# Queries and keys of ten head pairs made as block products in the gate phase and kept in device memory

## The chip, the cores and the metric

The kernel runs on one core of one Trainium2 chip. The metric is the device time of one execution in microseconds. Before the change three executions took 3416.34, 3417.03 and 3417.95 us, median 3417.03 us.

Names of engines: PE is TensorE, DVE is VectorE, ACT is ScalarE, POOL is GpSimd, SP is SyncE (it only issues DMAs here). Each runs its own instructions in order; they meet at semaphores.

## The reference, cut to what matters

A sequence of 1024 tokens of width 1024 goes through a first block (RWKV-7, mLSTM and a convolved FFN; untouched by the change) and then through two layers of a second block:

```python
h = rmsnorm_2(x, norm_g[layer])
u = h @ w_in[layer]
qa,ka,va,fa,za, qb,kb,vb,zb, qc,kc,vc,zc, ga,gb,gc = split(u)
ya = forgetting_attention(qa, ka, va, log_sigmoid(fa + b))      # 4 heads of 64, causal
ya = ya * silu(za)
yb = dilated_mixture_attention(rope(qb), rope(kb), vb) * silu(zb)   # 6 heads
yc = banded_attention(rope(qc), rope(kc), vc, 127, sinks) * silu(zc)  # 6 query heads on 2
merged = sigmoid(ga)*(ya @ w_br_a) + sigmoid(gb)*(yb @ w_br_b) + sigmoid(gc)*(yc @ w_br_c)
x = x + merged @ w_out[layer]
```

All is float32. The scores are scaled by 1/8 (head width 64).

## The kernel before

**Layout and precision.** Activations lie transposed: 128 channels on the partitions, 1024 tokens along the row, so a 1024-wide tensor is 8 such tiles (`xT`, 4 KB per partition each). A product of full precision is made of three products of halves: each operand is split in a high part (`hH`, `wH`) and the rest (`hL`, `wL`), and `wH*hH`, `wH*hL`, `wL*hH` are added in PSUM. POOL splits each weight tile (`split`, L683: `wH` at L688, `wL` at L690); a split waits until the product that used the buffer before is done.

**Plain column products.** `col_gemm` (L928, matmuls at L943) makes one tile of 128 output channels: 8 tiles of the input, 3 products, 2 halves of 512 tokens = 48 matmuls of 512 columns. It can run pieces of other work between its matmuls (`between`; the key is 3 x input tile + product, two matmuls each).

**Gate phase** (`gate_phase`: PE L1674, ACT L2588, DVE L3587). The 24 tiles of `ga, gb, gc` of a layer are made first: 4 plain, then 20 as `GATE_PAIRS` = 10 pairs. Such a pair takes the two output tiles, the two halves of the input channels and the two halves of the tokens as a 2x2 block product and makes it with 7 block products in place of 8 (`gate_products`, L1632): 7 x 4 tiles x 3 = 84 matmuls of 512 columns (L1650), with weight sums by POOL and ACT (`gate_high` L2541, `gate_low` L834). Per pair, ACT copies a seed (L2561), DVE adds and scales what comes out (L3639 to L3654), ACT applies the sigmoid (L2548), and SP stores the tile into device memory (`keep`). After pair 1 ACT also computes the logarithms of the forget gates (`gate_logs_of`, L2633 and L2635), which needs two other function tables. The block products use the second halves of the rows of `hH` and `hL` 0 to 3 as weight buffers, so ACT and DVE remake these halves after the last pair (L2607, L3670).

**Attention.** Heads are worked on two at a time: pairs A0, A1 (forgetting), B0, B1, B2 (dilated), C0 to C2 (band). A pair of A or B has four column products in PE's queue (`head_pair`, L1823), in the order query, key, value, gate z (the first pair A0: value, query, key, z). The end of the pair before (last transposes, last value products, reciprocal rows) is laid between the matmuls of the query product (`pair_end`, L1807). Between those of the z product lie the value transposes (L1708), the scores of the first 128 queries (`scores(0)`, L1740), and the first three of 8 periods: `period(n)` makes the scores of block n+1, transposes the probabilities of block n (L1767) and multiplies those of n-1 with the values (L1785). DVE takes bias and maximum of each score block (`maxima`, L3811), ACT the exponential (L2689). `period(0)` begins with `scores(1)`, which waits for both maxima of block 0.

**What DVE does ahead of the first maxima of a pair** (L3751), in its order: the output of the pair before (L3874); for A1 query scaling (L3724), scale and low part of the output before (`output_scale` L3736, `output_low` L3742, between them ACT's `yH` L2645), keys (L3730), two masks of the bias rows (L3776), the value copy (L3718). For B: rotary embedding of the query (L3709, L3712, L3714), `output_scale`, `output_low`, that of the keys, the value copy. Ahead of B0 it also scales the rotary tables (L3949, L3953). The half-turned copies that the embedding needs are made by ACT (raw copies L2638) and DMAs within SBUF (L2665). `output_scale` waits for reciprocals that go through device memory (L2657).

**SP's queue** after the gate phase is a plain loop of weight loads (L657).

## Time and profile before

| what | value |
| --- | --- |
| median of three executions | 3417.03 us |
| profiled execution, span from first to last instruction | 3412.5 us |
| what lies around the span, to the median | 4.5 us |
| PE busy | 3254.9 us, 95% |
| DVE, POOL, ACT busy | 58%, 48%, 31% |
| gate phase pairs, both layers | 1510 to 1717 us, 2480 to 2682 us |
| head pairs A0 to B2, both layers | 1717 to 2104 us, 2682 to 3069 us |

A row of a timeline or of the chain is one piece of work with its start and length in microseconds from the start of the span; in brackets stands how long the engine sat idle before it and what ended that. A row of windows gives for a stretch the busy time of each engine with the number of instructions in parentheses, then the granted TensorE clock as a share of 2.4 GHz. Matmul durations overlap: back to back, a 512-column matmul takes less than the duration shown for one.

### The profile page before, as it was taken

To read this page: it belongs to the slowest core of one execution; us is meant where nothing else is said; L and a number is where in the kernel's file an instruction comes from. 1 tells how busy PE (TensorE), PEld (TensorE's weight loads), DVE (VectorE), ACT (ScalarE), POOL (GpSimd) and SP (SyncE) were. 2 spreads that over 40 slices of the span, in tenths; PEclk is the share of its full clock that TensorE was granted. 3 is DMA by queue.
4 is the path that set the end of the run, shared out by engine and by line. 5 is a ranking of instruction groups with operands and counts; after the bars stand their busy time and mean duration, and the time that the engine had idled before them with its cause. 6 is when DMAs were issued, how large, how long until landed. Compare 5 with 4: busy or idle time off the path is not lost.

```text
span 3412.5 us, 55095 instructions
## 1 busy us (share of the span) xinstructions
PE 3254.9 (95%) x22070; PEld 2604.8 (76%) x22070; DVE 1971.0 (58%) x2678; ACT 1055.3 (31%) x1725; POOL 1622.7 (48%) x903
## 2 busy tenths in 40 slices
PE   7999789898999999999999999999999999999997
PEld 6878688687888888787877777678878877776786
DVE  7445644648877777883344554566752256444665
ACT  4212344223323333344332232320343233322301
POOL 3333334146777676657822222257478422222475
PEclk9999899999999999999999999999999999999998
DMA  3121100221111111112331211143223311111332
GB/s 137 44 91 44 56 4 4 85 83 53 53 55 41 54 55 55 50 62 99 143 107 44 56 52 47 38 163 121 99 105 106 119 45 50 43 44 50 136 124 87
DMA packets 88252, 247.68 MB, mean 73 GB/s; under 512 B 13072, under 2 KB 24048, under 8 KB 86144
## 3 DMA queue, kind: packets, MB, share of 16 engines
q1 hardware_dynamic: 69664, 189.34, 16.5%
q10 hardware_dynamic: 18400, 55.63, 5.0%
q8 instruction: 142, 2.33, 0.3%
q14 instruction: 46, 0.38, 0.0%
HBM read 191.28 MB, written 42.12 MB: 68 GB/s over the span
## 4 chain that ended last, share of the span: by engine, by line
PE 85%; DVE 8%; ACT 2%; issue 2%; POOL 2%; DMA 0%; DVEq 0%; POOLq 0%; SPq 0%; ACTq 0%
PE ps L943 30%; PE ps L1480 11%; PE ps L1650 9%; PE ps L1510 6%; PE ps L1934 5%; PE ps L1955 4%; PE ps L1740 3%; PE ps L1767 3%; PE ps L1785 3%; DVE sc L3811 2%; PE ps L1255 1%; PE ps L1533 1%; PE ps L1231 1%; PE ps L1618 1%; POOL unit_lo L834 1%
## 5 line engine op out<-in xcount | busy, mean ns | idle before, releaser
L688 POOL TENSOR_TENSOR wH<-wraw,pv 128x1024 fp32r<-128x1024 f32 x135 | 267.0, 1978 | 1221.5 <-PE ps L943 1097.7
L943 PE MATMUL ps<-hH,wH 128*128 128x512 f32 x1488 | 473.9, 400 | 26.3 <-DVE hL L3041 11.7
L943 PE MATMUL ps<-hL,wH 128*128 128x512 f32 x1488 | 466.6, 395 | 0.0
L943 PE MATMUL ps<-hH,wL 128*128 128x512 f32 x1488 | 465.2, 394 | 0.0
L3368 DVE TENSOR_TENSOR xT<-ps,xT 128x512 f32<-128x512 f32 x544 | 366.1, 690 | 60.9 <-PE ps L1510 54.8
L690 POOL TENSOR_TENSOR wL<-wraw,wH 128x1024 fp32r<-128x1024 f32 x135 | 353.7, 2620 | 10.6
L943 PEld LDWEIGHTS ps<-hH,wH 128*128 128x128 f32 x1488 | 274.5, 189 | 88.8 <-issue 17.9
L943 PEld LDWEIGHTS ps<-hL,wH 128*128 128x128 f32 x1488 | 277.8, 189 | 59.0 <-issue 1.7
L943 PEld LDWEIGHTS ps<-hH,wL 128*128 128x128 f32 x1488 | 277.7, 189 | 57.5 <-issue 0.3
L2689 ACT ACTIVATE sc<-sc,stat 128x256 f32<-128x256 f32 (+7 forms) x256 | 171.1, 669 | 163.1 <-DVE stat L3818 102.1
L1767 PE MATMUL ps<-cst,sc 128*128 128x128 f32 x900 | 148.7, 285 | 12.5 <-ACT pt L2709 8.4
L1767 PEld LDWEIGHTS ps<-cst,sc 128*128 128x128 f32 x900 | 97.0, 141 | 82.8 <-issue 60.7
L1740 PE MATMUL ps<-kP,qP 64*128 64x256 f32 (+3 forms) x672 | 131.6, 488 | 20.4 <-DVE stat L3818 16.6
L1650 PE MATMUL ps<-mixH,unit_hi 128*128 128x512 f32 x320 | 128.7, 402 | 14.5 <-POOL unit_lo L834 7.6
L1480 PE MATMUL ps<-mixH,unit_hi 128*128 128x512 f32 x336 | 133.8, 398 | 7.0 <-DVE ps L3483 4.1
L1480 PE MATMUL ps<-mixH,unit_lo 128*128 128x512 f32 x336 | 132.7, 395 | 0.0
L1480 PE MATMUL ps<-mixL,unit_hi 128*128 128x512 f32 x336 | 132.7, 395 | 0.0
L1650 PE MATMUL ps<-mixL,unit_hi 128*128 128x512 f32 x320 | 127.9, 400 | 0.0
L1650 PE MATMUL ps<-mixH,unit_lo 128*128 128x512 f32 x320 | 127.7, 399 | 0.0
L1785 PE MATMUL ps<-pt,vtok 128*64 128x128 f32 x1800 | 126.5, 280 | 0.0
L1510 PE MATMUL ps<-gL,wH 128*128 128x512 f32 x320 | 126.5, 395 | 0.0
L1510 PE MATMUL ps<-gH,wH 128*128 128x512 f32 x320 | 124.6, 389 | 0.0
(545 smaller groups left out, 7244.0 us busy)
## 6 DMA issues: line engine op xcount, KB each, us to landing
wraw<-ws SPq DMA_DIRECT2D x158, 512.0 KB, 3.5
gates<-gated SPq DMA_DIRECT2D x48, 512.0 KB, 2.7
sg<-gates SPq DMA_DIRECT2D x16, 1536.0 KB, 6.5
upA<-ws SPq DMA_DIRECT2D x42, 256.0 KB, 3.3
upB<-ws SPq DMA_DIRECT2D x42, 256.0 KB, 2.6
gateA<-ws SPq DMA_DIRECT2D x40, 256.0 KB, 3.5
gateB<-ws SPq DMA_DIRECT2D x40, 256.0 KB, 2.7
xT<-park ACTq DMA_DIRECT2D x2, 4096.0 KB, 12.1
```

The costliest lines, as they stand in the source:

```text
L688: pool.tensor_tensor(wH[:, j, :], wraw[:, j, :], zero, ALU.add).then_inc(w_hi, 1)
L690: pool.tensor_tensor(wL[:, j, :], wraw[:, j, :], wH[:, j, :], ALU.subtract).then_inc(w_ready[j], 1)
L943: mm = pe.matmul(pair(p)[:, half * HALF:(half + 1) * HALF], wp, hp[:, k, half * HALF:(half + 1) * HALF], start=(m == 0 and n == 0), stop=( ...
L1480: mm = pe.matmul(bank(b), wp, xp[:, k0 + k, c0:c0 + HALF], start=(start and k == 0 and n == 0), stop=(k == 3 and n == 2), skip_group_check ...
L1510: mm = pe.matmul(pair((2, 3, 1)[e % 3])[:, half * HALF:(half + 1) * HALF], w[:, 1, e * P:(e + 1) * P], h[:, half * HALF:(half + 1) * HALF] ...
L1650: mm = pe.matmul(bank(banks[b]), wp, xp[:, k0 + k, c0:c0 + HALF], start=(start and k == 0 and m == 0), stop=(k == 3 and m == 2), skip_grou ...
L1740: mm = pe.matmul(outs[j][:, c:e], qP[r, n * P:(n + 1) * P], kP[r, k0 + c - c0:k0 + e - c0], start=True, stop=True)
L1767: mm = pe.transpose(out[:, c:c + P], (SC[0] if br == "C" else SC[n % 2])[:, j, b + c:b + c + P], ident)
L1785: mm = pe.matmul(out[r, :], vtok[:, v + 64 * j:v + 64 * j + 64], pt[:, j, b + c:b + c + P], start=(c == c0), stop=(c + P == c1))
L1934: mm = pe.matmul(pair(p)[:, half * HALF:(half + 1) * HALF], wp, hp[:, k, half * HALF:(half + 1) * HALF], start=(k == k0 and n == 0), stop= ...
L2689: act.activation(buf[:, j, b + c0:b + c1], buf[:, j, b + c0:b + c1], ACT.Exp, bias=stat[:, S_NEG, s:s + 1], accum_out=stat[:, S_DEN, s:s + ...
L3368: ins = dve.tensor_tensor(x, bank(2 * pairs[e % len(pairs)] + half), x, ALU.add)
```

## The change

The queries and keys of pairs A0, A1, B0, B1, B2 are no longer plain column products in `head_pair`. They are made as `QK_PAIRS` = 5 more block pairs (one query and one key tile each) ahead of the 10 gate pairs, with the same 7 block products, stored to a tensor `qk` in device memory without the sigmoid, and loaded from there: into `qP` and `kP` for A (already scaled), and for B also, with the halves of each head swapped, into `turned` (four DMAs of 32 partitions each). `load_pair(n)` stands in SP's queue before the weight loads of the next pair and waits until all scores of the pair before are made; the A0 query is loaded during gate pair 1, its key after the last gate. A head pair then has two column products, value and z; the end of the pair before lies between the matmuls of the value product. DVE drops the query and key scaling of A and, for B, does both rotary embeddings first (`rope_loaded`), then `output_scale` and `output_low`. ACT drops its raw copies and in-SBUF swaps, and issues the bias-row DMAs of A0 at the end of the gate phase, ahead of remaking the halves of `hH`. In A0 the masks come before the value copy. In numbers per layer: 10 column products (480 matmuls) go, 35 block products (420 matmuls) come.

```diff
 PLAIN = 4
 GATE_PAIRS = (3 * KT - PLAIN) // 2
+QK_PAIRS = 5
+PAIRS = QK_PAIRS + GATE_PAIRS
 SLOT_GATES = 30
-LAYER_USES = 25
...
+
+    if n < QK_PAIRS:
+        return 2 + 4 * n, 3 + 4 * n
+    return gate_slot_of(PLAIN + 2 * (n - QK_PAIRS)), gate_slot_of(PLAIN + 2 * (n - QK_PAIRS) + 1)
 
...
+            def keep_second(L, n):
+                if n >= QK_PAIRS:
+                    keep(L, PLAIN + 2 * (n - QK_PAIRS) + 1)
+                    return
+                wait(sp, "g_in", L, PLAIN + 2 * n + 2)
+                if n < 2:
+                    wait(sp, "g_scaled", L, scaled(n))
+                else:
...
+
+            def keep_first(L, n):
+                if n >= QK_PAIRS:
+                    keep(L, PLAIN + 2 * (n - QK_PAIRS))
+                    return
+                wait(sp, "g_in", L, PLAIN + 2 * n + 1)
+                sp.dma_start(qk[2 * n], gated[0][:, :]).then_inc(sem("g_kept0"), 16)
+
+            def load_pair(L, n):
...
+
+                sp.wait_ge(sem("at_S"), (L * 8 + n) * 16)
+                for q, (dst, name) in enumerate(((qP, "q_in"), (kP, "k_in"))):
+                    sp.dma_start(dst[:, :], qk[2 * n + q]).then_inc(sem(name), 16)
+                    if n == 2 and q == 0:
+                        sp.wait_ge(sem("at_max"), (L * 8 + 1) * 16 + 18)
+                    if n >= 2:
+                        for a in range(4):
+                            b = a ^ 1
+                            sp.dma_start(turned[q][32 * a:32 * a + 32, :], qk[2 * n + q, 32 * b:32 * b + 32, :]
+                                         ).then_inc(sem(name), 16)
+
...
+                        sp.dma_start(qP[:, :], qk[0]).then_inc(sem("q_in"), 16)
+                    if n + 1 < PAIRS:
                         a, b = part(n + 1)
...
-                keep(L, 3 * KT - 1)
+                        wait(sp, "up_lo", L, PAIRS * UNITS)
+                        raw(1, u + 3, start + 5)
+                    keep_first(L, n)
+                keep_second(L, PAIRS - 1)
+                wait(sp, "g_in", L, PLAIN + 2 * PAIRS)
+                sp.wait_ge(sem("rows_ready"), L * 2 + 2)
+                wait(sp, "g_kept1", L, 16 * 3)
+                sp.dma_start(kP[:, :], qk[1]).then_inc(sem("k_in"), 16)
...
-                with sp.Fori(0, 12) as i:
+                for n in range(1, QK_PAIRS):
                     for j in range(2):
-                        sp.wait_ge(w_ready[j], i + (u + 5))
-                        sp.dma_start(wraw[:, j:j + 1, :], ws[bass.ds(i * 2 + (j + start + 6), 1)].rearrange("s p n -> p s n")
-                                     ).then_inc(raw_full[j], 16)
+                        raw(j, u + 3 + n, start + 4 * n + 4 + j)
+                    if n == 2:
+                        wait(sp, "g_kept0", L, 16 * (2 + PAIRS))
...
                         value_transposes(2)
 
                     def first_scores():
                         if br == "B":
                             pe.wait_ge(sem("a_rope"), L * 10 + i * 2 + 2)
-                        pe.wait_ge(sem("a_raw"), raw + 2)
+                        else:
+                            pe.wait_ge(sem("q_in"), since("q_in", loaded(L, br, i) + 16))
+                            pe.wait_ge(sem("k_in"), since("k_in", loaded(L, br, i) + 16))
                         scores(0)
...
+                    pieces = {4: value_tiles, 5: first_scores, 11: lambda: period(0), 16: lambda: period(1),
+                              21: lambda: period(2)}
...
-                        pe.wait_ge(sem("a_v"), L * 6 + 1)
-                        col_gemm(*slots[1], p=3)
-                        wait(pe, "a_free", L, GATE_PAIRS)
-                        col_gemm(*slots[3], p=1, between={2: value_tiles, 4: first_scores, 17: lambda: period(0),
-                                                          20: lambda: period(1), 22: lambda: period(2)})
...
+                        wait(pe, "g_in", L, PLAIN + 2 * PAIRS - 3)
+                        col_gemm(*slots[0], p=2, between={11: lambda: wait(pe, "half_lo", L, 4)}, first=4)
+                        wait(pe, "b_free", L, PAIRS - 1)
+                        wait(pe, "a_free", L, PAIRS - 1)
+                        col_gemm(*slots[1], p=1, between=pieces)
                     else:
                         col_gemm(*slots[0], p=0, between=ended)
-                        col_gemm(*slots[1], p=1)
-                        pe.wait_ge(sem("a_raw"), raw + 1)
-                        col_gemm(*slots[2], p=0)
-                        pe.wait_ge(sem("a_raw"), raw + 2)
-                        col_gemm(*slots[3], p=1, between={4: value_tiles, 5: first_scores, 11: lambda: period(0),
-                                                          16: lambda: period(1), 21: lambda: period(2)})
+                        col_gemm(*slots[1], p=1, between=pieces)
                 ends_here = br == "C" and i == 2
                 for n in range(within, 8 if ends_here else 7):
...
-                gate_sigmoid(L, PLAIN + 2 * n)
-                if n + 1 < GATE_PAIRS:
+                if n >= QK_PAIRS:
+                    gate_sigmoid(L, PLAIN + 2 * (n - QK_PAIRS))
+                if n + 1 < PAIRS:
...
-                    wait(act, "up_used", L, RING + GATE_PAIRS * UNITS - 3 + q)
+                wait(act, "up_used", L, RING + PAIRS * UNITS - 3)
+                bias_rows(L, 0)
+                for q in range(RING):
+                    k = ring_at(PAIRS - 1, q + 3)
+                    wait(act, "up_used", L, RING + PAIRS * UNITS - 3 + q)
                     act.activation(hH[:, k, HALF:T], xT[:, k, HALF:T], ACT.Copy, scale=norm_weight(L, k)
...
                 else:
                     slots = head_slots(L, br, i)
-                    if br == "B":
-                        act.wait_ge(gemm_done[0], slots[0][1] + 1)
-                        raw = L * 14 + i * 2 + 2 * first
-                        raw_copy(qraw2, 0, 0.125)
-                        swap_halves(qraw2, 0, raw + 1)
-                        output_hi(L, i + (first - 1))
-                        act.wait_ge(gemm_done[1], slots[1][1] + 1)
-                        raw_copy(kraw2, 1)
-                        act.wait_ge(sem("a_rot"), swaps(L, i * 2 + 1))
-                        swap_halves(kraw2, 1, raw + 2)
-                    if br == "A":
-                        for j in range(2):
-                            for q in range(2):
-                                spread(alternate(cM[q][:, j, :], 1 - q),
-                                       alternate(out[2 * i + j:2 * i + j + 1, L, :], 1 - q), L + 3)
+                    if br == "A" and i:
+                        bias_rows(L, i)
                     if br == "A" and i == 0:
                         first_values(L)
-                    if br == "A" and i:
+                    else:
+                        act.wait_ge(gemm_done[slots[0][0]], slots[0][1] + 1)
+                        act.activation(vst2[:, :], pair(0), ACT.Copy).then_inc(sem("a_v"), 1)
                         output_hi(L, i + (first - 1))
-                    if br == "B" or i:
-                        act.wait_ge(gemm_done[slots[2][0]], slots[2][1] + 1)
-                        if br == "B":
-                            act.wait_ge(sem("a_rope"), L * 10 + i * 2 + 1)
-                        act.activation(vst2[:, :], pair(0), ACT.Copy).then_inc(sem("a_v"), 1)
                 def unmask(n):
...
-                    dve.tensor_tensor(ga[:, HALF:T], c, grows[:, HALF:T], ALU.mult).then_inc(sem("g_in"), 1)
+                    exit_first(ga[:, HALF:T], c, 1).then_inc(sem("g_in"), 1)
                     wait(dve, "up_used", L, used + 7)
...
+                    if n < 2 or n >= QK_PAIRS:
+                        dve.tensor_tensor(gb[:, 0:HALF], a, grows[:, 0:HALF], ALU.mult).then_inc(sem("a_free"), 1)
+                    else:
+                        dve.tensor_copy(gb[:, 0:HALF], a).then_inc(sem("a_free"), 1)
                     wait(dve, "a_free", L, n + 1)
                     dve.sem_inc(sem("g_in"), 1)
...
+            def rope_loaded(L, n, q, done):
+
+                step, dst, turn = n * 2 + (L + 1) * 2, (qP, kP)[q][:, :], turned[q][:, :]
+                name = ("q_in", "k_in")[q]
+                dve.wait_ge(sem(name), since(name, done))
+                dve.tensor_tensor(dst, dst, ropeT[:, 0, :], ALU.mult).then_inc(sem("rope_step"), 1)
+                dve.tensor_tensor(turn, turn, ropeT[:, 1, :], ALU.mult).then_inc(sem("rope_step"), 1)
+                dve.wait_ge(sem("rope_step"), step + 2)
+                dve.tensor_tensor(dst, dst, turn, ALU.add).then_inc(sem("a_rope"), 1)
...
-                        queries(L, i)
-                        output_scale(L, i + (first - 1))
-                        output_low(L, i + (first - 1))
-                        keys(L, i)
                 if br == "B":
-                    for q, raw, dst in ((0, qraw2, qP), (1, kraw2, kP)):
-                        rope(L, L * 10 + i * 2 + q, L * 14 + i * 2 + (2 * first + 1 + q), swaps(L, i * 2 + (q + 1)),
-                             SC[1][:, q, :], SC[1][:, q, :], raw, dst)
-                        if q == 0:
-                            output_scale(L, i + (first - 1))
-                            output_low(L, i + (first - 1))
+                    for q in range(2):
+                        rope_loaded(L, L * 10 + i * 2 + q, q, loaded(L, br, i) + 80)
+                if br == "B" or (br == "A" and i):
...
```

The rest adjusts counts of semaphores and uses (`LAYER_USES` 25 to 20) and the order in which the four half rows are remade.

## Rows read from the trace of the kernel before

**Rows 1.** The page, section 1: busy us, share of the span and instructions per engine.

```profile
PE 3254.9 (95%) x22070; PEld 2604.8 (76%) x22070; DVE 1971.0 (58%) x2678; ACT 1055.3 (31%) x1725; POOL 1622.7 (48%) x903
```

**Rows 2.** Windows of core 0: stretch, its us, then busy us (instructions) per engine, granted clock.

```profile
1570.00:1717.00 147.00, 146.17 (x640) 120.62 (x640) 54.32 (x57) 53.21 (x81) 115.22 (x82) 0.99 0.37 131
```

**Rows 3.** Timeline of DVE, gate phase, first layer: start us, us, operation, idle before.

```profile
1610.51 0.70 DVE L3639 TENSOR_TENSOR ps<-ps,ecopy 128x512 f32<-128x512 f32 x1 [5.01 <-PE ps L1650]
...
1629.55 0.70 DVE L3639 TENSOR_TENSOR ps<-ps,ecopy 128x512 f32<-128x512 f32 x1 [5.52 <-PE ps L1650]
```

**Rows 4.** Timelines of ACT and PE around gate pair 2, both layers.

```profile
1563.55 1.28 ACT L2548 ACT_TABLE_LOAD   x1
...
1566.32 0.58 ACT L2561 ACTIVATE ps<-ps 128x512 f32<-128x512 f32 x1
...
1566.95 0.80 PE L1650 MATMUL ps<-mixH,unit_hi 128*128 128x512 f32 x1 [4.43 <-ACT ps L2561]
...
2533.32 0.50 PE L1650 MATMUL ps<-mixH,unit_hi 128*128 128x512 f32 x1 [2.49 <-ACT ps L2561]
```

**Rows 5.** Windows of PE alone after two such gaps: us, PE busy (matmuls), granted clock.

```profile
1567.00:1572.30 5.30, 5.30 (x13) 0.51 0.73 254
...
2533.30:2537.60 4.30, 4.28 (x13) 0.67 0.71 257
```

**Rows 6.** Chain that ended last, head pairs A0, A1, B0: start us, us, what, count.

```profile
1717.67 34.24 PE ps L943 x150
...
1799.52 29.51 PE ps L943 x130
...
1830.79 2.95 PE ps L943 x12
...
1875.55 29.51 PE ps L943 x130
```

**Rows 7.** Timeline of DVE at the start of head pair A1.

```profile
1799.43 1.23 DVE L3874 SCALAR_TENSOR_TENSOR ypair<-ps,sz 128x1024 f32<-128x1024 f32 x1 [3.05 <-PE ps L1785]
...
1806.18 1.94 DVE L3736 TENSOR_TENSOR ypair<-ypair,recT 128x1024 f32<-128x1024 f32 x1
...
1809.34 2.12 DVE L3742 TENSOR_TENSOR yL<-ypair,yH 128x1024 fp32r<-128x1024 f32 x1 [1.22 <-ACT yH L2645]
...
1818.92 3.41 DVE L3776 TENSOR_TENSOR cMo<-cMe,cst 128x1024 f32<-128x1024 f32 x1
...
1829.94 1.23 DVE L3718 TENSOR_TENSOR vtok<-ps,pv 128x1024 f32<-128x1024 f32 x1 [7.61 <-PE ps L1708]
...
1831.57 0.29 DVE L3811 CUSTOM_DVE_ANT_0 sc<-ps,cMe 128x128 f32<-128x128 f32 x1
```

**Rows 8.** Timeline of POOL in the same stretch: weight tile of the next product.

```profile
1805.15 1.89 POOL L688 TENSOR_TENSOR wH<-wraw,pv 128x1024 fp32r<-128x1024 f32 x1 [32.07 <-PE ps L943]
...
1807.12 3.26 POOL L690 TENSOR_TENSOR wL<-wraw,wH 128x1024 fp32r<-128x1024 f32 x1
```

**Rows 9.** Timeline of DVE at the start of head pair B0.

```profile
1884.46 3.10 DVE L3709 TENSOR_TENSOR qP<-qraw,ropeT 128x1024 f32<-128x1024 f32 x1 [0.23 <-DVE ropeT L3953]
...
1888.96 1.23 DVE L3714 TENSOR_TENSOR qP<-qP,sc 128x1024 f32<-128x1024 f32 x1
...
1890.10 1.22 DVE L3736 TENSOR_TENSOR ypair<-ypair,recT 128x1024 f32<-128x1024 f32 x1
...
1892.72 2.31 DVE L3742 TENSOR_TENSOR yL<-ypair,yH 128x1024 f32 x1 [1.40 <-ACT yH L2645]
```

**Rows 10.** Timeline of ACT's queue: a bias-row DMA of A0 in each layer.

```profile
1730.34 5.85 ACTq L2079 DMA_DIRECT2D cMo<-out  x1
...
2684.29 0.76 ACTq L2079 DMA_DIRECT2D cMo<-out  x1
```

**Rows 11.** DMA issues: issuer, count, KB each, median us from issue to landing.

```profile
xT<-park ACTq DMA_DIRECT2D x2, 4096.0 KB, 12.1
...
cMo<-out ACTq DMA_DIRECT2D x8, 256.0 KB, 6.6
```

More of the change, by code:

```diff
@@ L599, in part @@
                 def part(n):
-                    return [start + gate_slot_of(PLAIN + 2 * n + q) for q in range(2)]
+                    return [start + slot for slot in pair_slots_of(n)]
                 raw(0, u + 1, start + gate_slot_of(1))
@@ L614, in gate_loads @@
                     keep(L, n)
-                for n in range(GATE_PAIRS):
-                    keep(L, PLAIN - 1 + 2 * n)
-                    if n + 1 < GATE_PAIRS:
+                for n in range(PAIRS):
+                    if n:
+                        keep_second(L, n - 1)
+                    else:
+                        keep(L, PLAIN - 1)
+                    if n == QK_PAIRS + 1:
+                        sp.wait_ge(sem("gate_rows"), L + 5)
+                        wait(sp, "g_kept0", L, 16 * 3)
+                        sp.dma_start(qP[:, :], qk[0]).then_inc(sem("q_in"), 16)
+                    if n + 1 < PAIRS:
                         a, b = part(n + 1)
@@ L896, in _ @@
                 first_gate_units(L, 0)
-                for n in range(GATE_PAIRS):
+                for n in range(PAIRS):
                     later_gate_units(L, n)
@@ L1692, in gate_phase @@
                 col_gemm(0, u + 2, p=2, freed=RING)
-                for n in range(GATE_PAIRS):
+                for n in range(PAIRS):
                     gate_products(L, n)
@@ L2598, in gate_phase @@
                 gate_sigmoid(L, 1)
-                for n in range(GATE_PAIRS):
+                for n in range(PAIRS):
                     gate_period(L, n)
@@ L2614, in gate_phase, with bias_rows @@
                 act.wait_ge(sem("x_moved"), L * 32 + 272)
+            def bias_rows(L, i):
+                for j in range(2):
+                    for q in range(2):
+                        spread(alternate(cM[q][:, j, :], 1 - q), alternate(out[2 * i + j:2 * i + j + 1, L, :], 1 - q), L + 3)
             def store_scaled(part):
@@ L2623, in first_values @@
                 act.wait_ge(gemm_done[0], first_use(L) + 4)
[L2624 to L2626 removed]
+                act.activation(vst2[:, :], pair(2), ACT.Copy).then_inc(sem("a_v"), 1)
+                wait(act, "g_kept0", L, 16 * (2 + PAIRS))
+                wait(act, "g_kept1", L, 16 * (2 + PAIRS))
                 act.dma_start(ropeT[:], rope).then_inc(sem("tables"), 16)
@@ L3632, in gate_phase @@
                 low(3, 3, 3)
-                for n in range(GATE_PAIRS):
+                for n in range(PAIRS):
                     a, b, c, e = [bank(q) for q in gate_banks(n)]
@@ L3667, in gate_phase @@
                             scale_residual(k, 0, HALF)
-                for q, k in enumerate((2, 3, 0, 1)):
+                for q in range(RING):
+                    k = ring_at(PAIRS - 1, q + 3)
                     wait(dve, "half_hi", L, q + 1)
@@ L3672, in gate_phase @@
                 if L == 0:
-                    for k in (2, 3, 0, 1):
+                    for k in range(RING):
                         scale_residual(k, HALF, T)
@@ L3782, in head_pair @@
                     value_copy(2, L * 6 + i + first)
-                if br == "A" and not i:
-                    mask_bias()
                 def maxima(n):
@@ L3967, in layer_loop @@
                 if L < LAYERS - 1:
-                    merge_add(L, LAYER_ROWS - 1, 1, first_use(L) + 24, pairs=range(4), low=L + 1)
+                    merge_add(L, LAYER_ROWS - 1, 1, first_use(L) + LAYER_USES - 1, pairs=range(4), low=L + 1)
                 else:
```

153 lines of the change are left out of this document (76 added, 77 removed).

## The prediction

> **What bounds the kernel now.** The page comes first: PE is busy 95% of the span [rows 1], and the chain that ended last runs through it in both stages that the change touches [rows 6]; so time is PE's matmuls plus the few places where PE waits. Then the two stages. In the gate phase from 1570 to 1717 us PE is busy 146.17 of 147 us at a granted clock of 0.99, POOL 115, DVE 54, ACT 53 [rows 2]: PE-bound. One pair takes 1629.55 - 1610.51 = 19.04 us [rows 3], for 84 matmuls 0.2267 us each. In the head pairs the chain of waits shows where cover lies: A1's first three products and the start of the fourth run without a gap, 130 matmuls in 29.51 us (0.227 each) [rows 6]. In that time DVE, ACT and the queues do what must precede the first maxima. That cover is what the change removes.
>
> **What PE gains.** 10 products of 48 matmuls go per layer, 5 block pairs of 84 come. Per pair 96 x 0.2267 = 21.76 us go and 19.04 come: 2.72 us, and 27.2 us over ten pairs, if neither stage waits longer than before. That sum has to be corrected in both stages.
>
> **Gate phase.** The new pairs have POOL's and PE's work of a gate pair, less of ACT's (no sigmoid) and of DVE's (pairs 2 to 4 drop one operation). The scaled copies out of PSUM stand in no row; nearest is the 0.70 us addition with 5.01 us of idle before it [rows 3], so anything up to some 2 us costs nothing and I take nothing. 10 x 19.04 = +190.4 us.
> One stall shrinks. After pair 1 ACT takes a table load at 1563.55, a sigmoid and one weight copy before the seed at 1566.32, and PE sits idle 4.43 us until that seed, 2.49 in the second layer [rows 4]. With pair 1 a query-key pair, load and sigmoid go from this place: the seed comes 2.77 us earlier, less 0.52 for the copy, 2.25. The reload moves to pair 5, where ACT has slack. After the idle the granted clock is 0.51 for 5.3 us, 13 matmuls where 23 fit; in the second layer 0.67 over 4.3 us [rows 5]. That is the 1.2 GHz level, costing 5.3 - 13 x 0.227 = 2.35 us and 1.35 us. With idle of 2.2 and 0.2 us left I count 1.0 and 1.35 saved. Together -(2 x 2.25 + 1.0 + 1.35) = -6.9 us; bounds -4.5 and -8.2.
>
> **Head pairs, method.** Let s be the moment when PE resumes after the end of the pair before (1799.52 for A1). Today `scores(1)`, the head of period 0, goes at 1830.79 + 2.95 = 1833.74, s + 34.2 [rows 6]; its maxima were ready at 1831.57 + about 0.6 [rows 7]. From there to the next s it takes 1875.55 - 1833.74 = 41.8 us [rows 6], bound by this chain, which the change leaves. So each pair saves exactly what `scores(1)` moves forward. PE alone would reach it at: 24 matmuls left of the value product 5.44, 10 of z 2.27, transposes and scores of block 0 with two matmuls 1.75, 12 matmuls 2.95: s + 12.4, a move of 21.8.
>
> **DVE sets it instead.** An operation of 1024 columns lasts 1.23 us; one that waits for nothing starts 1.14 after the one before (1888.96 to 1890.10) [rows 9], and I count 1.27 for a dependent one. The embedding of a tile is three, the last dependent: 3.6. One price lies in the split of the next value weights, which POOL starts once the value product ends, s + 5.63, in two operations [rows 8]. A DVE operation that reads two SBUF tiles and falls on one of them takes 1.94, 2.12, 3.41 us in place of 1.23; each ends about 1.1 us after POOL's ends (1807.04 to 1808.12) [rows 7, 8]. So they alternate, each waiting for the other whole.
> The Trainium skill says this in "SBUF — State Buffer", section "Who interferes with whom": two SBUF inputs against a GpSimd read is an exclusive lock, the second blocks fully. By the rule a B pair loses the whole split, 4.3 us; without a lock it would lose nothing (the first rival). The trace agrees with the rule.
>
> *A1.* `output_scale` cannot start before the reciprocals, s + 6.1, and today runs 1.94; `output_low` ends at 1809.34 + 2.12, s + 11.9 [rows 7], both as today. Two masks 2.3 (clear of POOL), value copy, and from its start 2.2 to the second maximum (1829.94 to about 1832.1) [rows 7]: s + 16.55. Moves 17.65.
> *B0.* The table scaling keeps DVE until 1884.46, and the query's first product takes 3.10, under the split [rows 9]; both stay. The embedding ends at 1890.1, s + 14.6. Now the keys' follow, 3.6 (no split any more), then scale to start of low 2.62 (1890.10 to 1892.72) [rows 9], low 1.15, value copy to maximum 2.2: s + 24.2. Moves 10.0.
> *B1, B2.* DVE is free at s + 1.05 (end of L3874) [rows 7]. Query 3.6 to s + 4.6, keys 3.7 plus the 4.3 us of the split: s + 12.3. Scale to low 2.6, low 1.15, copy to maximum 2.2: s + 18.3. Moves 15.9 each.
> *A0.* No pair ends before it. From 1717.67 PE needs 10.9 for value, 2.27 + 1.75 + 2.95 for the rest to `scores(1)`: 1735.5, then 41.8: the next s at 1777.3 against 1799.52 [rows 6], 22.2. In the first layer DVE's last residual scaling ends about 1 us later, since the halves of `hH` wait behind four DMA issues, 0.76 us each in the second layer [rows 10], and POOL's split of the z weights waits for it: 0.8 off, 21.4. Value copy and maxima keep up there, masks being first. ACT's issue is the open cost: one of these DMAs held the queue 5.85 us in the first layer [rows 10], behind a large store that now comes later. If it still does, PE waits up to 3.5 us for the halves, once; if not, nothing. I take nothing, for the queue in front is empty.
> Saved: first layer 21.4 + 17.65 + 10.0 + 31.8 = 80.85, second 81.65: -162.5 us.
>
> **Loads.** 2 MB per B pair are issued when the last scores of the pair before are made, some 14 us before s. 4 MB landed in 12.1 us, 256 KB bias rows in 6.6 [rows 11]; so they land before DVE wants them, with some 5 us to spare for B1 and B2, and I take nothing; if ten issues queue badly, some 3 us at each of six pairs.
>
> **Clock.** PE now idles some 4 us before `scores(1)` of A1 and in two pieces in every B pair (9 us at once in B0). Gaps of 2.49 and 4.43 us were each followed by the lower level, at 1.35 and 2.35 us [rows 4, 5]. Eight such places; each costs 0 to 2.35, as the slow matmuls may end before the maxima anyway. I take 0.6: +4.8; bounds 0 and 18.8.
> The Trainium skill's "TensorE: Matmul & The Clock Gate", section "Part 1: The HAM clock gate (the "warmup" mystery)", holds that idleness lowers the clock by half and activity must win it back; by it the upper half of these bounds is the likelier.
>
> **Sum.** +190.4 - 6.9 - 162.5 + 4.8 = +25.8 us, on the span 3412.5 and the 4.5 us around it up to the median 3417.0: 3442.8 us. Bounds of this case: the smallest terms (no clock loss, -8.2, a microsecond less on each of eight pairs) give 3429, the largest (12 for clock, 7 for ACT's queue) 3457.
>
> **Rivals.** *The lock does not bite:* the order of POOL and DVE falls so that the split hides. Then B1, B2 reach `scores(1)` at s + 14.2 and A1 at 14.4: 4 x 4.1 + 2 x 2.1 = 20.6 less, and less idle, no clock loss: 3417.4, no change. For it: DVE waits for PE before L3874 (3.05 us in A1), so the order may fall differently; against: three operations of rows 7 met a split and all are long.
> *DVE keeps up, the other side:* one mechanism, DVE's chain after s fits in PE's 12.4 us, decided at that point. Then 27.2 + 6.9 - 0.8 = 33.3 us are gained: 3383.7. If it fits half-way, the gain starts when the waits of a layer stay under 17 us (I have 28). For it: DVE is only 58% busy [rows 1], and A0 shows the form; against: nine operations and ACT's round trip stand in line, 11 us without any lock.
> *Late loads or a lasting low clock:* a further 18 us at six B pairs (3 each): 3461.
> *The tiles are not made cheaper:* if a pair in the longer phase took over 21.8 us, PE would lose too; the interval of rows 3 holds within 0.2 us in 12 of the 18, and the others have their causes in ACT or POOL, so I give this no share of its own.
>
> **How the numbers follow.** Forecast 0.64, lock absent 0.10, DVE keeps up 0.14, late loads or low clock 0.12. The forecast's own range is 3429 to 3457; to leave out no more than 2 in 10 the range is 3412 to 3458, the case at 3384 and half of the slowest outside. A measurement here tells 0.2%, 6.8 us, from no change. Slower by more: 0.64 + 0.12 + 0.02 = 0.78; within: 0.08; faster: 0.14.
>
> **What would show it.** Block pairs 19.04 us apart within 0.2, save those with a known stall, and PE idle before pair 2 near 2.2 us and under 1. From s to `scores(1)`: 16.5 in A1, 24 in B0, 18 in B1 and B2; PE waiting there on DVE (L3811's successor), not on a DMA. DVE without idle between its output and the first maxima. A clock under 1.00 in head pairs, where it was 1.00. The forecast is wrong if `scores(1)` comes at s + 12 to 14, if PE's wait in a B pair ends on `q_in` or `k_in`, or if a block pair takes over 20 us.

## The result, and the profile after

The changed kernel takes **3447.56 us** (median of four, 3438.58 to 3450.88) against 3416.71 for the kernel before beside it: ratio **1.0085**, 95% interval 1.0071 to 1.0099. It is slower. Forecast were 3442.8 us and slower with 0.78. The first profiled execution is its fastest (span 3436.5 us at a mean clock of 0.982); a second profile of the same kernel, taken later, has a span of 3446.2 at 0.979, like the other three executions of the first set (3445.5 to 3448.9). Both are used below.

The page of the first, section 1, answers [rows 1]:

```profile
PE 3233.8 (94%) x21950; PEld 2585.4 (75%) x21950; DVE 1991.7 (58%) x2724; ACT 1096.9 (32%) x1803; POOL 1677.7 (49%) x973
```

PE's busy time went down by 21.1 us, and the span up by 24.0: 45 us more in which PE waits. Where that is, the starts of the same instructions in both traces tell. "Seed" is DVE's addition of a block pair [rows 3], s is PE's start after the end of the pair before.

| stretch, first + second layer | before | first profile | second | forecast |
| --- | --- | --- | --- | --- |
| start to first seed | 1518.56 | -2.57 | +0.34 | 0 |
| seeds of pair 0 to pair 2 | 53.86 + 47.05 | -7.61, -3.27 | -3.26, -3.30 | -3.25, -3.6 |
| pair 2 to the last pair | 134.41 + 133.79 | +95.13, +94.86 | +95.27, +94.85 | +95.2 each |
| last seed to s of A1 | 92.69 + 92.77 | -18.81, -22.29 | -18.83, -22.22 | -21.4, -22.2 |
| A1 | 76.03 + 75.99 | -16.29, -15.11 | -16.32, -16.30 | -17.65 each |
| B0 | 76.18 + 76.18 | -9.99, -10.35 | -10.00, -10.37 | -10.0 each |
| B1 | 76.24 + 76.24 | -14.80, -14.82 | -13.54, -13.64 | -15.9 each |
| B2 | 76.24 + 76.25 | -14.78, -14.80 | -14.09, -14.15 | -15.9 each |
| the rest of both layers | 730.02 | -0.50 | -0.74 | 0 |
| sum | 3412.5 | +24.0 | +33.7 | +25.8 with 4.8 for the clock |

**Gate phase.** Two seeds of DVE and one window of 147 us, which answer [rows 3] and [rows 2]:

```profile
1600.32 0.70 DVE L3704 TENSOR_TENSOR ps<-ps,ecopy 128x512 f32<-128x512 f32 x1 [5.01 <-PE ps L1716]
1619.36 0.70 DVE L3704 TENSOR_TENSOR ps<-ps,ecopy 128x512 f32<-128x512 f32 x1 [5.86 <-PE ps L1716]
```

```profile
1656.00:1803.00 147.00, 147.00 (x650) 121.74 (x650) 42.84 (x52) 53.59 (x82) 105.54 (x81) 1.00 0.36 123
```

19.04 us apart, as before, and nothing else binds there. PE's timeline ahead of pair 2 in each layer answers [rows 4]; 2.2 and 0.2 us of idle were forecast:

```profile
1559.18 0.50 PE L1716 MATMUL ps<-mixH,unit_hi 128*128 128x512 f32 x1 [2.06 <-ACT ps L2622]
...
2541.56 0.50 PE L1716 MATMUL ps<-mixH,unit_hi 128*128 128x512 f32 x1 [0.41 <-ACT ps L2622]
```

**Head pairs.** PE's timeline, first profile, where it waits longest: A1, B0, B1.

```profile
1881.95 0.70 PE L1806 MATMUL ps<-kP,qP 64*128 64x256 f32 x4 [3.82 <-DVE stat L3876]
...
1943.36 0.80 PE L1806 MATMUL ps<-kP,qP 64*128 64x128 f32 x4 [8.86 <-DVE kP L3797]
...
2009.59 0.80 PE L1806 MATMUL ps<-kP,qP 64*128 64x256 f32 x2 [4.74 <-DVE stat L3876]
```

The releaser is DVE each time, never `q_in` or `k_in`. With s at 1865.66, 1925.40 and 1991.59, `scores(1)` comes at s + 16.3 in A1 and s + 18.0 in B1 (and B2); in B0 it comes at s + 24.2, after the first scores at s + 18.0. DVE's timeline between, A1 and B1 (it answers [rows 7, 9]):

```profile
1872.08 2.18 DVE L3803 TENSOR_TENSOR ypair<-ypair,recT 128x1024 f32<-128x1024 f32 x1 [5.28 <-DMA recT<-out]
1875.48 2.12 DVE L3809 TENSOR_TENSOR yL<-ypair,yH 128x1024 fp32r<-128x1024 f32 x1 [1.22 <-ACT yH L2716]
1877.52 1.21 DVE L3836 TENSOR_TENSOR cMe<-cMo,cst 128x1024 f32<-128x1024 f32 x1
1878.66 1.21 DVE L3836 TENSOR_TENSOR cMo<-cMe,cst 128x1024 f32<-128x1024 f32 x1
1879.79 1.21 DVE L3786 TENSOR_TENSOR vtok<-ps,pv 128x1024 f32<-128x1024 f32 x1
...
1997.30 1.22 DVE L3795 TENSOR_TENSOR turned_k<-turned_k,ropeT 128x1024 f32<-128x1024 f32 x1
1998.56 2.80 DVE L3797 TENSOR_TENSOR kP<-kP,turned_k 128x1024 f32<-128x1024 f32 x1
2001.28 3.41 DVE L3803 TENSOR_TENSOR ypair<-ypair,recT 128x1024 f32<-128x1024 f32 x1
2006.09 1.23 DVE L3809 TENSOR_TENSOR yL<-ypair,yH 128x1024 f32 x1 [1.40 <-ACT yH L2716]
2007.23 1.22 DVE L3786 TENSOR_TENSOR vtok<-ps,pv 128x1024 f32<-128x1024 f32 x1
```

POOL's timeline beside B1 (answers [rows 8]):

```profile
1997.28 2.99 POOL L754 TENSOR_TENSOR wH<-wraw,pv 128x1024 fp32r<-128x1024 f32 x1 [32.03 <-PE ps L1009]
2000.35 3.25 POOL L756 TENSOR_TENSOR wL<-wraw,wH 128x1024 fp32r<-128x1024 f32 x1
```

**Clock.** Windows of PE after `scores(1)`: us, busy (matmuls), granted clock; the last two numbers are DMA share and GB/s. A1 in the first profile, then B1 in the second, where s + 18.0 is 2016.93:

```profile
1881.90:1883.20 1.30, 1.25 (x8) 0.94 0.00 0
1883.20:1886.20 3.00, 3.00 (x9) 0.50 0.00 0
1886.20:1889.20 3.00, 3.00 (x18) 0.96 0.00 0
```

```profile
2012.20:2016.90 4.70, 0.03 (x1) 0.91 0.00 0
2016.90:2020.90 4.00, 3.97 (x12) 0.50 0.00 0
2020.90:2022.90 2.00, 2.00 (x6) 0.51 0.00 0
2022.90:2026.90 4.00, 4.00 (x23) 1.00 0.00 0
```

The level is 1.2 GHz for some 3 us after the wait in one, 6 in the other. From `scores(1)` to the next s it took 41.9 us before the change in A1 and 42.0 in the B pairs. Now it takes 43.4 in B1 and B2 of the first layer in the first profile and 44.7 and 44.2 in the second; A1 takes 43.4 as well, but 44.6 in the second layer of the first profile. In B0 it stays 42.0.

### The profile page after: what moved, and what is told of

Same layout as the page of the kernel before. It is cut to its first block and busy times, and to the rows that moved or that the text cites. A ratio compares the mean times of both kernels' runs of the same rounds, so it can differ in the third digit from the quotient of the medians.

```text
span 3436.5 us, 54966 instructions
## 1 busy us (share of the span) xinstructions
PE 3233.8 (94%) x21950; PEld 2585.4 (75%) x21950; DVE 1991.7 (58%) x2724; ACT 1096.9 (32%) x1803; POOL 1677.7 (49%) x973
## 3 DMA queue, kind: packets, MB, share of 16 engines
q8 instruction: 144, 2.36, 0.3%
## 5 line engine op out<-in xcount | busy, mean ns | idle before, releaser
L1009 PE MATMUL ps<-hH,wH 128*128 128x512 f32 x1168 | 381.4, 408 | 29.0 <-DVE hL L3096 12.4
L1009 PE MATMUL ps<-hL,wH 128*128 128x512 f32 x1168 | 372.9, 401 | 0.0
L1009 PE MATMUL ps<-hH,wL 128*128 128x512 f32 x1168 | 369.8, 398 | 0.0
L1009 PEld LDWEIGHTS ps<-hH,wH 128*128 128x128 f32 x1168 | 218.0, 193 | 80.6 <-issue 21.1
L1716 PE MATMUL ps<-mixH,unit_hi 128*128 128x512 f32 x480 | 188.1, 392 | 10.0 <-POOL unit_lo L900 7.4
L1716 PE MATMUL ps<-mixH,unit_lo 128*128 128x512 f32 x480 | 187.5, 391 | 0.0
L1716 PE MATMUL ps<-mixL,unit_hi 128*128 128x512 f32 x480 | 187.4, 390 | 0.0
L1833 PE MATMUL ps<-cst,sc 128*128 128x128 f32 x900 | 149.9, 287 | 12.5 <-ACT pt L2780 8.4
L900 POOL TENSOR_TENSOR unit_lo<-gateA,unit_hi 128x512 fp32r<-128x512 f32 x90 | 130.8, 1466 | 48.5 <-ACT unit_hi L2602 43.6
L1716 PE MATMUL ps<-hH,unit_hi 128*128 128x512 f32 x360 | 140.2, 389 | 0.7 <-DVE gated L3651 0.7
L1546 PE MATMUL ps<-mixH,unit_hi 128*128 128x512 f32 x336 | 133.2, 396 | 8.0 <-DVE ps L3538 5.1
L1716 PE MATMUL ps<-hH,unit_lo 128*128 128x512 f32 x360 | 140.1, 389 | 0.0
L1716 PE MATMUL ps<-hL,unit_hi 128*128 128x512 f32 x360 | 140.1, 389 | 0.0
```

Source lines behind the costliest of these rows:

```text
L900: pool.tensor_tensor(unit_lo[s][:, :], src, unit_hi[s][:, :], ALU.subtract).then_inc(sem("up_lo"), 1)
L1009: mm = pe.matmul(pair(p)[:, half * HALF:(half + 1) * HALF], wp, hp[:, k, half * HALF:(half + 1) * HALF], start=(m == 0 and n == 0), stop=( ...
L1546: mm = pe.matmul(bank(b), wp, xp[:, k0 + k, c0:c0 + HALF], start=(start and k == 0 and n == 0), stop=(k == 3 and n == 2), skip_group_check ...
L1716: mm = pe.matmul(bank(banks[b]), wp, xp[:, k0 + k, c0:c0 + HALF], start=(start and k == 0 and m == 0), stop=(k == 3 and m == 2), skip_grou ...
L1833: mm = pe.transpose(out[:, c:c + P], (SC[0] if br == "C" else SC[n % 2])[:, j, b + c:b + c + P], ident)
```

## The experiments

In all, s is as above, and the length of a pair is the time from one s to the next. The kernel before took 3415.26 us (median) beside the first four, 3413.22 beside the next four and 3413.79 beside the last two.

### The changed kernel again

> The changed kernel once more, with nothing changed. Its profiled execution had a span of 3436.5 us at a mean granted clock of 0.982, its three others 3445.5 to 3448.9 at 0.979 and 0.978. If the difference lies in how long TensorE stays at its lower level after the waits in the head pairs, the span again moves with the clock, the waits themselves (A1 3.8, B0 8.9, B1 and B2 4.7 us) repeat within 0.1 us, and the stretch from scores(1) to the next s takes 43.5 us in some pairs and up to 46 in others, where it took 41.9 before the change. If the difference lies elsewhere (loads, the gate phase), these stretches repeat within 0.2 us and another stage is 9 to 12 us longer.

**3448.0 us** (3443.68 to 3449.29), ratio 1.0095 (1.0081 to 1.0110). The waits repeat within 0.05 us (3.82, 8.86, 4.70). B1 and B2 are 1.2 and 0.7 us longer per layer, all of it behind `scores(1)`, but no stretch there reaches the 46 us that were thought possible. The larger part of the difference between the two profiles lies elsewhere: in the first layer PE waits 3.31 us for POOL in gate pair 0 in each trace, and after the same wait the clock differs. Windows of PE right behind it: before, first profile, second profile.

```profile
1535.40:1540.40 5.00, 4.97 (x12) 0.50 0.52 210
```

```profile
1532.80:1537.80 5.00, 4.94 (x22) 1.00 0.00 2
```

```profile
1535.70:1540.70 5.00, 4.93 (x12) 0.50 0.00 0
```

So about 4.4 us of the gain that the first profile shows ahead of pair 2 were luck with the clock and no effect of the change; the second profile gives this term as it was forecast. Of the 9.7 us between the profiles 4.4 lie here, 2.9 in the stretch ahead of the first seed (its cause was not looked for), and the rest is made up of the lines of the table from A1 to B2.

### POOL's split later

```diff
-                splits((u + 4) * 2, (u + 13) * 2)
+                for use in range(u + 4, u + 13):
+                    if u + 5 <= use <= u + 8:
+                        pool.wait_ge(sem("at_max"), (L * 8 + use - u - 4) * 16 + 4)
+                    for j in range(2):
+                        split(j, use, False)
```

> Only POOL's order is changed: the split of the next value weights waits until the first two maxima of the running pair are made, so no POOL operation lies beside DVE's chain after s. Theory (POOL and DVE exclude each other): DVE's operations that took 1.94 to 3.41 us take 1.23; scores(1) goes from s + 16.3 to 14.4 in A1, from 24.2 to 22.3 in B0, from 18.0 to 14.2 in B1 and B2: 11.3 us per layer, 22.6 in all, and where PE then waits under 2 us the 1.6 us at the lower clock go too, 3 places a layer: 3415 to 3425 us. Rival (those operations are long for a reason of their own): the times of scores(1) stay and the kernel takes 3447 us.

**3414.32 us**, ratio 1.0000 (0.9991 to 1.0008): 33.7 us less than the changed kernel on the same chip, level with the kernel before, and 0.7 us below the range expected. DVE's timeline in B1, and POOL's, which now waits for DVE:

```profile
1996.20 1.22 DVE L3801 TENSOR_TENSOR kP<-kP,turned_k 128x1024 f32<-128x1024 f32 x1
1997.34 1.22 DVE L3807 TENSOR_TENSOR ypair<-ypair,recT 128x1024 f32<-128x1024 f32 x1
1999.96 1.22 DVE L3813 TENSOR_TENSOR yL<-ypair,yH 128x1024 f32 x1 [1.40 <-ACT yH L2720]
```

```profile
2003.49 1.89 POOL L754 TENSOR_TENSOR wH<-wraw,pv 128x1024 fp32r<-128x1024 f32 x1 [40.58 <-DVE stat L3880]
```

2.80 and 3.41 became 1.22, and `scores(1)` of B1 and B2 comes at s + 14.2, as expected. A1 comes to 15.1 (14.4 expected: `output_scale` waits until s + 7.1 for its reciprocals). B0 comes to 20.8 (22.3 expected): the table scaling too had stood beside the split, 6.50 us with it and 4.90 without. B1 and B2 take 56.1 to 57.8 us instead of 62.1 to 62.7. The rival falls: the long operations are long because of POOL. Of the 36.4 us between the traces of this run and the one above, 24.4 are `scores(1)` coming earlier in eight pairs; another 10.0 are clock, since with shorter waits the stretches behind `scores(1)` lose 2.9 us in all where they lost 12.9.

### Output operations later

```diff
-                if br == "B" or (br == "A" and i):
-                    output_scale(L, i + (first - 1))
-                    output_low(L, i + (first - 1))
+                later = br == "B" or (br == "A" and i)
...
+                    if n == 0 and later:
+                        output_scale(L, i + (first - 1))
+                    if n == 1 and later:
+                        output_low(L, i + (first - 1))
```

(ACT's `output_hi` moves behind its exponentials of block 1.)

> Only DVE's and ACT's order is changed: output_scale and output_low of the pair before (and ACT's copy between them) come after the first and second period of A1, B0, B1 and B2, as the window branch has them, not ahead of the first maxima. Theory (DVE's serial chain sets scores(1)): A1 comes to s + 12.4 to 14.0 (the masks wait for their bias rows), B0 to s + 20.1, B1 and B2 to PE's own s + 12.4, if the two operations fit into later gaps of DVE; 17.6 to 19.2 us per layer, with 1.6 at the lower clock in three places: 3400 to 3412 us. Rival (the work is only moved and delays the periods by as much): scores(1) comes forward but the stretch from there to the next s grows from 43.5 by 3 to 4 us, and the kernel stays at 3440 to 3448.

**3414.96 us**, ratio 1.0003 (0.9994 to 1.0012): 33 us less than the changed kernel, though 3 us above the range expected. B1 and B2 come to `scores(1)` at s + 13.2 (PE still waits 0.66 us for the embedded keys ahead of its first scores) and take 55.2 us: the stretch behind it is 42.0 again, so the moved operations cost nothing in the periods, and that rival falls. B0 gains only 1.1 and 0.6 us where 4.1 were expected. Its PE waits 8.87 us for the embedded keys (windows of PE in it, and from the first scores to `scores(1)`):

```profile
1937.50:1946.30 8.80, 0.03 (x1) 0.64 0.00 0
1946.40:1951.40 5.00, 5.00 (x16) 0.62 0.00 0
```

After this wait PE itself needs 5.1 us for the 12 matmuls and four scores up to `scores(1)`, at the lower clock, and so DVE's saved time is not what ends last. In A1 the masks now wait for their bias rows (DVE's timeline), and `scores(1)` comes at s + 14.3:

```profile
1882.12 1.28 DVE L3835 TENSOR_TENSOR cMe<-cMo,cst 128x1024 f32<-128x1024 f32 x1 [8.63 <-DMA cMo<-out]
```

### Embedding earlier

The scaling of the tables moves too, in three pieces, from the start of B0 into A0, and DVE's loop over the B pairs is written out; that part of the diff is left out here.

```diff
-                    for q in range(2):
-                        rope_loaded(L, L * 10 + i * 2 + q, q, loaded(L, br, i) + 80)
+                    rope_loaded(L, L * 10 + i * 2 + 1, 1, loaded(L, br, i) + 80)
...
                     if n == 7:
                         reciprocals()
+                        if br == "A" and i == 0:
+                            scale_tables(L, 0)
+                        following = (0 if br == "A" and i == 1 else i + 1 if br == "B" and i < 2 else None)
+                        if following is not None:
+                            rope_loaded(L, L * 10 + following * 2, 0, loaded(L, "B", following) + 80)
```

> Only DVE's order is changed: the scaling of the table tiles goes into gaps of A0, and the embedding of the next B pair's queries into the gap of 5.6 us before the last copy of the pair before; the keys' stay after s. Theory (serial chain): B0, B1 and B2 come to scores(1) at s + 14.1, A1 stays at 16.3; 10.1 + 3.9 + 3.9 = 17.9 us per layer, 36 in all, and a part of the lower clock's 1.6 us: 3402 to 3412 us. Rival (late loads): the queries land after the gap and the embedding then delays the last copy, so that s comes 1 to 3 us later in each pair and half of the gain is lost: 3420 to 3430.

**3403.84 us**, ratio 0.9969 (0.9958 to 0.9981): faster than the kernel before. B0, B1 and B2 are alike, `scores(1)` at s + 14.0, 55.85 us. DVE's timeline at the end of A1 shows that the loads only just allow it, as DVE waits 2.64 us for one:

```profile
1923.97 1.22 DVE L3795 TENSOR_TENSOR qP<-qP,ropeT 128x1024 f32<-128x1024 f32 x1 [2.64 <-DMA turned_q<-qk]
...
1927.51 1.22 DVE L3906 COPY pt<-ps 128x1024 f32<-128x1024 f32 x1
1931.16 1.22 DVE L3945 SCALAR_TENSOR_TENSOR ypair<-ps,sz 128x1024 f32<-128x1024 f32 x1 [2.43 <-PE ps L1851]
```

The copy of the last block comes when the embedding ends, and A1's stretch to the next s is 43.4 us as without the edit. The late-load rival falls here too, if not by much.

### PE's waits filled with matmuls

`fill` runs in front of `period(0)` and, in B0, of `first_scores`. PE's loop over the B pairs is also written out, pair by pair.

```diff
+                    def fill(count):
+                        for _ in range(count):
+                            pe.matmul(bank(6), wH[:, 1, 0:P], hH[:, 0, 0:HALF], start=True, stop=True)
```

> The changed kernel with matmuls put into PE's waits whose result nobody reads (written to a PSUM bank that the pair's first output product overwrites): 16 before period 0 of A1, 20 before that of B1 and B2, 39 before the first scores of B0, at 0.227 us each as long as the waits of 3.8, 4.7 and 8.9 us. Nothing that the pairs wait for is changed. Theory (the lower clock after a wait is a cost of its own): scores(1) stays where it was within 0.3 us, the granted clock of the head pairs is 1.00, and the stretch from scores(1) to the next s is 41.9 us in place of 43.4 to 44.7 in A1, B1 and B2: 4.7 to 7.8 us per layer, 3432 to 3438 us where the changed kernel takes 3447.8, with a narrower spread. Rival (the waits alone cost): 3447 us or a little more.

**3438.82 us**, ratio 1.0074 (1.0060 to 1.0087). The unfilled kernel ran on another chip: against its 3448.0 this is 9 us less, but each set against the kernel before beside it, 25.6 us more in place of 32.7, it is 7, and the two intervals overlap. The lengths of the pairs are the surer measure. `scores(1)` stays at s + 16.3 and 18.0. PE's window behind B1's `scores(1)` (s + 18.0 is 2014.22):

```profile
2014.20:2018.20 4.00, 3.98 (x20) 1.00 0.00 0
```

20 matmuls where there were 12. The stretch is 41.9 us in A1 and 42.0 in B1 and B2; these pairs give 12.8 us against the second profile. B0 loses 1.6 per layer: with its first wait filled, the second grows from 1.0 to 2.8 us (0.8 to 2.4 in the second layer), and now the lower clock follows that one. The sum is 9.5 us less, and the time 0.8 above the range expected. So the lower clock is a cost of its own, on top of waits that did not change.

### Output operations later, on the kernel before

The same edit of order as in the third experiment:

```diff
-                        output_scale(L, i + (first - 1))
-                        output_low(L, i + (first - 1))
                         keys(L, i)
...
+                    if n == 0 and later:
+                        output_scale(L, i + (first - 1))
+                    if n == 1 and later:
+                        output_low(L, i + (first - 1))
```

> The kernel before, with output_scale, output_low and ACT's copy put after the first periods, as in the experiment that gained 33 us on the changed kernel. Theory (the two query-key products were cover for just this work): nothing is gained, as PE has 30 us of products before the first maxima; pairs 76.03 and 76.24 us apart, 3415 us. Rival (the order is better in itself): a gain of 5 us or more here too.

**3414.37 us**, ratio 1.0005 (0.9995 to 1.0014). Nothing. Its pairs stay 76.03 to 76.24 us long. An order worth 33 us behind two column products is worth nothing behind four. The other orders (split later, embedding earlier) were not run on the kernel before. That they would gain nothing in these pairs is argued from its trace alone: PE comes to each `scores(1)` of A1 to B2 without any wait, at s + 34.2.

### The orders together

The edits of the third and the fourth in one kernel.

> The changed kernel with the output operations after the first periods and the queries' embedding in the gap of the pair before; POOL's order as it was. Theory (serial chain in front of PE's own 12.4 us): A1 at s + 14.3, B0, B1 and B2 at PE's own s + 12.4 to 13.2, where no clock is lost, pairs 54.3 to 55.2 us apart; from 3403.8 some 17 us less, 3383 to 3390. Rival (the moved operations meet in the pair's later gaps, and the period chain grows): pairs stay over 55.8 and the time at 3400.

**3386.54 us**, ratio 0.9921 (0.9908 to 0.9935). B0, B1 and B2 come to `scores(1)` at PE's own s + 12.4 and take 54.25 us. A1 comes at s + 14.5 and 14.9; in the second layer the lower clock costs 2.8 us after its wait of 2.44 us, and the pair takes 59.5 us.

Then also the second, and in ACT's gate phase:

```diff
-                wait(act, "up_used", L, RING + PAIRS * UNITS - 3)
-                bias_rows(L, 0)
                 for q in range(RING):
...
+                bias_rows(L, 0)
                 act.activation(arows[:, :], grows[:, :], ACT.Copy).then_inc(sem("rows_ready"), 1)
```

> All of it: output operations later, table scaling and queries' embedding earlier, POOL's split of the next value weights after the first maxima, and in the gate phase ACT's four bias-row issues behind the copies of the last half of h (for the 2.1 us that PE waits for the z weights in A0 of the first layer). Theory: scores(1) at PE's own s + 12.4 everywhere, pairs 54.3 apart, no clock under 1.00 there: 3380 to 3384 us, which is the time of the rival of the prediction in which DVE keeps up. Rival: as in the run beside it, A1 alone moves by 1.9 us a layer: 3 to 4 us under it and no more.

**3382.54 us**, ratio 0.9912 (0.9897 to 0.9927). DVE's timeline at the start of B0, where the value copy now waits for PE, and PE's at `scores(1)`, which no longer waits:

```profile
1928.21 1.22 DVE L3802 TENSOR_TENSOR kP<-kP,turned_k 128x1024 f32<-128x1024 f32 x1
1933.44 1.22 DVE L3790 TENSOR_TENSOR vtok<-ps,pv 128x1024 f32<-128x1024 f32 x1 [4.00 <-PE ps L1778]
```

```profile
1937.17 0.70 PE L1810 MATMUL ps<-kP,qP 64*128 64x256 f32 x4
```

This is the prediction's rival "DVE keeps up", made true in B0, B1 and B2. In A1 it is not: `scores(1)` comes at s + 14.4 and 14.2, not at the 12.4 expected, and keeps 1.7 to 2.0 us of wait, on the bias rows. So the gain is 30.7 us against the kernel before beside it, not the rival's 33.3; that the time lies so near its 3383.7 is in part luck, as the kernel before took 3413.2 here and not the 3417.0 that the prediction starts from. The bias-row issues behind the copies cut A0's wait for the z weights in the first layer from 2.1 to 0.8 us, but the next wait there, for ACT's copy of the values, grew from 0.6 to 1.7: A0 became 0.2 us shorter, and this edit is worth next to nothing. Nor is the later split shown to add much: between the traces of the two runs A1 of the second layer alone makes 3.5 us, where a wait of 1.69 us is not followed by the lower clock.

> The version with all four changes of order once more, beside the next one on the same chip: 3380 to 3385 us, A1 at s + 14.2 to 14.4 with a wait of 1.7 to 2.0 us, B0, B1 and B2 at s + 12.4.

**3384.61 us**, ratio 0.9913 (0.9899 to 0.9926). In the first layer A1 is as expected; in the second its bias rows land later, and `scores(1)` comes at s + 15.1 after a wait of 2.67 us. Beside it, the masks split:

```diff
-                if br == "A":
+                if br == "A" and i == 0:
                     mask_bias()
                 if br != "C":
                     value_copy(2, L * 6 + i + first)
+                if br == "A" and i:
+                    mask_bias((0,))
...
                 maxima(0)
+                if br == "A" and i:
+                    mask_bias((1,))
```

> The same, and in A1 DVE copies the value tiles before it masks the bias rows, and masks the second tile only after the first two maxima. Theory (what is left of A1's wait is two masks and a copy queued behind a bias-row DMA that lands some 10 us after s): A1 comes from s + 14.3 to 12.4, pair 54.3 us instead of 56.2, so 3.8 us in all, 3376 to 3380 us. Rival (the mask itself comes too late, since the rows land at s + 10): scores(1) at s + 13 or later, and 2 us or less are gained.

**3383.59 us**, ratio 0.9911 (0.9897 to 0.9925). DVE in A1:

```profile
1880.74 1.23 DVE L3790 TENSOR_TENSOR vtok<-ps,pv 128x1024 f32<-128x1024 f32 x1 [6.28 <-PE ps L1778]
1882.15 1.23 DVE L3851 TENSOR_TENSOR cMe<-cMo,cst 128x1024 f32<-128x1024 f32 x1 [0.19 <-DMA cMo<-out]
```

`scores(1)` comes at s + 12.5 (12.4 in the second layer), and A1 takes 55.2 and 54.3 us where the run beside it has 56.1 and 57.6. That is 4.2 us in the traces, but the profiled execution of the run beside it was the slowest of its five, and between the medians lies only 1.0, which is within the spread of either (5.3 and 3.7). The 3376 to 3380 us expected were not reached; whether it is a gain stays open. Both versions are 29 to 30 us, 0.9%, faster than the kernel before.

## Why the prediction was right, and where it was off

- *Slower, because the column products were cover for DVE.* Right. Putting the output operations later is worth 0 on the kernel before and 33 us on the changed one, and with DVE's chain out of the way in all pairs but A1 the time is 3382.5.
- *Block pairs, +190.4.* +190.0 and +190.1.
- *The stall ahead of pair 2, -6.9.* -6.6 in the second profile. -10.9 in the first, of which 4.4 is the clock in pair 0.
- *`scores(1)` at s + 16.55, 24.2, 18.3.* Measured 16.3, 24.2 (23.8 in the second layer) and 18.0. The terms of A1 and B0 held one by one. That of B1 holds a slip: its 4.6 + 3.7 + 4.3 are 12.6 and not 12.3, so its terms give 18.6; the split cost less than taken (below). In B0 it is DVE's chain that ends last, as forecast, but barely. PE's row there, first profile:

```profile
1949.60 0.70 PE L1806 MATMUL ps<-kP,qP 64*128 64x256 f32 x4 [0.73 <-DVE stat L3876]
```

  After the first scores at s + 18.0 PE itself is busy, in part at the lower clock, until s + 23.5 (23.2 in the second profile). The forecast left this out. It is why a shorter chain of DVE behind the keys gains only 0.6 to 1.1 us there.
- *POOL's split, 4.3 us in a B pair, 2.1 in A1.* B1 and B2 moved by 3.8 when it was taken away, A1 by 1.2, B0 by 3.4 to 3.5 (the table scaling had met a split as well). Here the Trainium skill's rule in "SBUF — State Buffer", section "Who interferes with whom" (a DVE operation with two SBUF inputs and a GpSimd read exclude each other) is what the run shows.
- *A0, 21.4 in the first layer.* 18.8: the split of the z weights came later than the 0.8 us taken for it. PE waits 2.1 us for it, since POOL's first operation took 3.95 us beside DVE's two masks, where 1.89 is usual, and another 0.8 us for ACT's copy of the values, behind the store of x. The forecast had counted neither of these.
- *Clock, +4.8.* **The step that was mis-sized.** Over A1, B1 and B2 of both layers the stretches behind `scores(1)` are longer than their 41.9 or 42.0 by 12.9 us in the second profile (1.5, 2.7, 2.2 and 1.6, 2.7, 2.2), 10.3 in the first; with the waits filled these places gave back 12.8. The 0.6 a place rested on "the slow matmuls may end before the maxima anyway". That is so in B0 alone. In the others the wait ends with `scores(1)` itself, and all that runs slowly comes behind it, on the path. The difference of 8.1 is that between the forecast's +25.8 and the second profile's +33.7, but for other terms of up to 2.6 us that cancel. That the first profile's +24.0 lies nearer is luck, the 4.4 us in gate pair 0 among it. The Trainium skill's "TensorE: Matmul & The Clock Gate", section "Part 1: The HAM clock gate (the "warmup" mystery)", was read in the prediction as pointing to the upper half of the bounds, 9.4 to 18.8 us; with 12.9 that was the better guide.
- *Rivals.* The lock bites. DVE does not keep up by itself. The tiles are as cheap as before. No wait of PE or DVE ends on a load of queries or keys in the changed kernel.

## What to carry to other kernels

Before PE's work is made cheaper, list what the other engines do beside it that the next wait needs. What PE saves becomes a gain only as far as this chain is shorter than the work that PE has left. Here 27 us of matmul time saved cost 31 us, and changes of order, of which the one tried on the kernel before was worth nothing there, turned this into a gain of 30. A wait that appears on PE is to be priced with its tail: here the lower clock cost 1.4 to 2.8 us, 2.1 in the mean, on top of each wait of 3.8 to 4.7 us whose end was next on the path, and nothing in B0, where another wait hid it.

## What the runs showed of the hardware that was not expected

- After equal waits the lower clock came in one place and not in another. In the run with the later split, B1 and B2 of the first layer both wait 1.69 us before `scores(1)`. Windows of the next 4 us, B1 and B2:

```profile
2003.50:2007.50 4.00, 4.00 (x20) 1.00 0.00 0
2059.70:2063.70 4.00, 4.00 (x14) 0.62 0.00 0
```

  and the 3.31 us in gate pair 0 was followed by 1.00 once and by 0.50 twice. In the head pairs of the changed kernel it came after every wait of 3.8 us and more, and in another run also after 2.44 us, where it cost as much as anywhere (2.8 us). What decides is not shown.
- Both sides pay where POOL and DVE meet: POOL's two operations took 1.89 and 2.36 us alone, and 2.99 and 3.25 beside DVE's (3.95 for the first beside the two masks in A0).
